# A prompt attention stage with its output projection in two 512-column halves instead of four 256-column quarters

## The chip, the cores and the metric

The kernel runs on one core of a Trainium2 chip. The metric is the device time of one execution in microseconds; three executions of the kernel before gave 1206.93, 1207.19 and 1207.43. The rows below come from one further execution that the hardware profiler recorded.

## The reference, cut to what matters

One decoder layer for a prompt of 1,024 tokens and for 64 sample tokens (8 sequences of 8), with 1,024 channels. A combined input projection feeds a pooling mixer (512 channels) and a sparse attention (8 heads of 64); both outputs are joined, projected and added to the input:

```python
u, q, k, v, qi, ki, wi = project(rms_norm(hp, norm_mix_g[l]), w_in[l])
pool_o = pool_mix(u_ext, 0, pool_w[l], pool_scale[l])
attn_o = dsa_prompt(q, k, v, qi, ki, wi)
hp = hp + jnp.concatenate([pool_o, attn_o], axis=-1) @ w_out[l]
hp = hp + hier_moe(rms_norm(hp, norm_ffn_g[l]), *moe_args)
```

The sample tokens go the same way. The output projection of the prompt, the product with `w_out` in the fourth line, is what the change touches: 1,024 tokens x 1,024 inputs x 1,024 outputs, in float32.

## The kernel before

The stages follow each other: input projections and indexer scores, the index of the sample tokens, **the prompt's attention with its output projection**, the attention of the sample tokens, the experts, the final norm. The change lies in the third, which the profile shows from about 387 to 679 us.

**Work in that stage.** The prompt is cut into tiles of 128 tokens, i = 0 to 7; NT = 8 stands for the 64 sample tokens. Each tile has four pairs of heads, h = 0 to 3, called heads below, and for each pair the two key groups g = 0 and 1. A list `tasks`, written out by a loop, is the order in which PE works; the other engines follow it too, except that they take the turn T(h,1) ahead of the scores S (`tasks_elsewhere`). The tasks are:

- S(i,h): scores of one head pair against 128 (i+1) keys (line 1264) into PSUM banks 0 to 3. DVE adds the mask and takes the maximum (L2369, L2372), ACT takes the exponential (L1799). S is issued one head ahead: S(i,h+1) lies between T(i,h,0) and T(i,h,1).
- T(i,h,g): PE transposes the probabilities in chunks of up to four blocks into banks 4 and 5 in turn (L1275), and ACT copies each chunk out (L1552). From tile 4 on a T has two chunks.
- V(i,h): the probabilities times the values, into bank 6 (L1287). It waits until ACT has copied all chunks of T(i,h,0) and T(i,h,1). Behind V(i,3) DVE inverts the row sums and ACT copies bank 6 out.
- OT(i): PE turns the inverse sums into bank 7 (L1301), and DVE multiplies the attention outputs by them (L2300) into `mixA`, the projection's operand.
- OP(i,q): the output projection of tile i (L1317), eight products of 128 x 128 with a slice of `w_out`, each two records in the trace, into bank 7; DVE adds the result to the residual (L2310). For the sample tokens, OP(8,0 to 3) takes the pooled half alone (four products of 64 rows); OP(8,4) and OP(8,5) take the other half with 512 columns in the next stage (L1311 and L2306).
- SQ(i): ACT squares the sum and takes the root (L1779, L1781), with a load of a table before the root and another before the next exponential. NM(i): DVE normalises (L2315, L2319). XR(i,0), XR(i,1): PE transposes the normalised tile into bank 7 (L1322) and ACT copies it. LG(i): router logits (L1328) into bank 7, which DVE adds up (L2164).

All tasks that use bank 7 (OT, OP, XR, LG) hand it over: the next one starts when the last one's result has been taken out. Every engine works in order. DVE has another job in between: the selection of the sample tokens' keys, cut into pieces (L2017 is the long one), four of them behind every S of tiles 1 to 6; `PIECES` fixes them by S and V and not by OP. GpSimd's L954 and L956 wait for the last of them.

**Where OP stood.** Behind T(i,h,1) and ahead of V(i,h): the quarter 0 of tile i-1 in head 1, 1 in head 2, 2 in head 3, and quarter 3 of tile i-2 in head 0. OT(i-1) and SQ(i-2) follow V(i,0), NM(i-2) follows V(i,1), XR(i-2,0) V(i,2), XR(i-2,1) stands behind T(i,3,0), LG(i-2) behind V(i,3). Behind the last tile a closing list is written out by hand. SP stores the sum h(i) when `last_op(i)` has been added and the normalised tile behind NM(i), and then loads the residual of tile i+2.

Of the kernel before, what the change touches and what calls it, by code (L numbers as in the profile page):

```python
# [18 lines left out]
ALU = mybir.AluOpType  # L19
# [7 lines left out]
NT = SEQ // P  # L27
# [99 lines left out]
def program(nc, x_prompt, x_sample, cache_k, cache_v, cache_idx_k, state_pool, page_table, norm_mix_g, w_in,  # L127
# [5 lines left out]
    with ctx:  # L133
# [6 lines left out]
        ps = ctx.enter_context(nc.psum_tensor("ps", [P, 8, 512], F32))  # L140
# [83 lines left out]
        wout = cut(8 * D, (8, D))  # L224
# [15 lines left out]
        hb = cut(2 * D, (2, D))  # L240
# [28 lines left out]
        hbS = mixP[0:SR, :, 0:256]  # L269
# [150 lines left out]
        for n in range(TILES + 1):  # L420
# [4 lines left out]
            if n:  # L425
                order += [("T1", ("qi", n - 1)), ("T0", ("k", n - 1))]
                i = ORDER[n - 1]
# [39 lines left out]
            return "PT0" if t == ("OP", NT, 5) else "M"  # L467

        def last_op(i):
            return ("OP", i, 3) if i < NT else ("OP", NT, 5)  # L470

        tasks = step("S", 0)
        for i in range(NT):
            for h in range(PAIRS):
                out, old = i - 1, i - 2
                turned, summed, later = [], [], []
                if out >= 0:
                    summed += {0: [], 1: [("OP", out, 0)], 2: [("OP", out, 1)], 3: [("OP", out, 2)]}[h]
                    later += {0: [("OT", out)]}.get(h, [])
                if old >= 0:  # L480
                    turned += {3: [("XR", old, 1)]}.get(h, [])
                    summed += {0: [("OP", old, 3)]}.get(h, [])
                    later = {0: [("SQ", old)], 1: [("NM", old)], 2: [("XR", old, 0)], 3: [("LG", old)]}[h] + later
                tasks += [("T", i, h, 0)] + turned + step("S", i * PAIRS + h + 1) + [("T", i, h, 1)]
                tasks += summed + [("V", i, h)] + later
        i = NT - 1
        tasks += [("OP", i - 1, 3), ("SQ", i - 1), ("OT", i), ("OP", i, 0), ("NM", i - 1), ("OP", i, 1), ("XR", i - 1, 0),
                  ("OP", i, 2), ("XR", i - 1, 1), ("OP", i, 3), ("LG", i - 1), ("SQ", i), ("OP", NT, 0), ("NM", i), ("OP", NT, 1),
                  ("XR", i, 0), ("OP", NT, 2), ("XR", i, 1), ("OP", NT, 3), ("LG", i)]
        tasks_elsewhere = list(tasks)  # L490
        for n, t in enumerate(tasks):
            if t[0] == "S" and n:
# [53 lines left out]
        filled, emptied, use = {}, {}, {}  # L546
# [24 lines left out]
        def take(eng, tag, q, key):  # L571

            eng.wait_ge(filled[tag + q], use[tag, q, key] + 1)
# [464 lines left out]
        def _(pe):  # L1038
            mm = nc.tensor.matmul
# [141 lines left out]
            for n in range(TILES + 1):  # L1181
                if n == 3:
                    pe.wait_ge(state_in, 16)
                    claim(pe, "1", "T0", "state")
                    for g in range(4):
                        ins = tr(ps[:, 0, g * SB * HALO:(g + 1) * SB * HALO], stt_in[0:SB * HALO, g * P:(g + 1) * P], ident(SB * HALO))
# [104 lines left out]
            def tail(t):  # L1291
                kind, i = t[0], t[1]
                r = rows(i)
# [8 lines left out]
                elif kind == "OP":  # L1302
# [11 lines left out]
                    last = 3 if i == NT else 7  # L1314
                    for k in range(last + 1):
                        lhs = mixP[:, k, tok] if k < 4 else mixA[:, k - 4, :]
                        ins = mm(ps[0:r, 7, 0:256], lhs, wout[:, k, 256 * t[2]:256 * t[2] + 256], start=(k == 0), stop=(k == last))  # L1317
                elif kind == "XR":
                    pe.wait_ge(x2_ready, i + 1)
                    for j in range(4):  # L1320
# [621 lines left out]
        def _(dve):  # L1942
            v = nc.vector
# [348 lines left out]
            def tail(t):  # L2292
                kind, i = t[0], t[1]
                r, s = rows(i), i % 2
                if kind == "OT":
                    take(dve, "2b", "M", t)
                    dve.wait_ge(o_kept, i + 1)
                    if i:
                        take(dve, "2b", "M", ("OP", i - 1, 3))
                    v.tensor_tensor(mixA[:, :, :].rearrange("p b q -> p (b q)"), ps[:, 7, :], Osb, ALU.mult).then_inc(emptied["2bM"], 1)  # L2300
                elif kind == "OP":
                    take(dve, "2b", part_of(t), t)
# [3 lines left out]
                        v.tensor_tensor(part, new, part, ALU.add).then_inc(emptied["2b" + part_of(t)], 1)  # L2306
                        return
                    dve.wait_ge(xr_in[s], 16 * (i // 2 + 1))
                    part = hbS[:, t[2], :] if i == NT else hb[0:r, s, 256 * t[2]:256 * t[2] + 256]
                    v.tensor_tensor(part, ps[0:r, 7, 0:256], part, ALU.add).then_inc(emptied["2bM"], 1)  # L2310
                elif kind == "NM":
                    dve.wait_ge(std2_ready, i + 1)
                    if i == 0:
# [233 lines left out]
```

## Time and profile before

| | |
|---|---|
| median of three executions | 1207.19 us |
| the profiled execution, its own time | 1207.76 us |
| its span in the profile | 1205.9 us |
| PE busy in the span | 1084.2 us (90%), 6212 matmul records |
| DVE, ACT, POOL busy | 562.5, 415.3, 233.1 us |
| projection of the prompt and the sample's first half (L1317) | 544 records, 125.6 us |
| mean granted PE clock | 0.954 |

PE is TensorE, PEld its weight loads, DVE VectorE, ACT ScalarE, POOL GpSimd, SP SyncE, and SPq the queue on which SP issues transfers. A row of a timeline gives the start in us from the span's start, the time from the first to the last of its instructions in us, engine, line, operation, what is written and read, how many, and in brackets how long the engine sat idle before it and what released it. A matmul's end is modelled, and a row of several lasts a little longer than the time until the next task starts on PE; so the text takes the pace of PE from starts.

### The profile page before, as it was taken

How to read it: one execution, taken by the hardware profiler on the slowest of the kernel's cores; microseconds unless marked ns; L12 is line 12 of the kernel's file. 1: busy time of each engine (PE TensorE's matmuls, PEld its weight loads, DVE VectorE, ACT ScalarE, POOL GpSimd, SP SyncE). 2: the span in 40 equal slices, each digit the busy share in tenths (PEclk: the TensorE clock that was granted, in tenths of full speed). 3: DMA queues.
4: the chain of work that ended last, by engine and by line, in shares of the span. 5: the costliest groups of instructions: out<-in, count | busy, mean ns of one | idle time of the engine just before them, and what ended most of it. 6: DMA issues, size and time to landing. Idle time of an engine off the chain costs nothing. (4 is left out here: it accounts for less than half of the span.)

```text
span 1205.9 us, 16395 instructions
## 1 busy us (share of the span) xinstructions
PE 1084.2 (90%) x6212; PEld 733.0 (61%) x6212; DVE 562.5 (47%) x1273; ACT 415.3 (34%) x976; POOL 233.1 (19%) x270
## 2 busy tenths in 40 slices
PE   4999989899877899999998799679999999999980
PEld 2554433354444577777776465467778788787860
DVE  3234568999997877666562263111311111111114
ACT  1234445567534355555551143311011111111114
POOL 1433224354422000000004110011212112121210
PEclk9999999999989699999999889879999999999995
DMA  6510000010084111110111472379999999999928
GB/s 219 200 46 12 6 28 1 1 35 5 1 231 154 44 54 53 54 44 28 37 53 61 190 304 84 123 273 348 326 334 343 335 337 346 332 345 333 296 32 304
DMA packets 51198, 191.42 MB, mean 159 GB/s; under 512 B 10910, under 2 KB 13806, under 8 KB 40885
## 3 DMA queue, kind: packets, MB, share of 16 engines
q1 hardware_dynamic: 39439, 142.71, 33.2%
q0 software_dynamic: 11536, 47.71, 14.0%
q8 instruction: 38, 0.62, 0.2%
q14 instruction: 27, 0.22, 0.1%
q10 hardware_dynamic: 158, 0.16, 0.1%
HBM read 162.49 MB, written 28.19 MB: 158 GB/s over the span
## 5 line engine op out<-in xcount | busy, mean ns | idle before, releaser
L1476 PEld LDWEIGHTS ps<-mem 128*128 128x128 f32 x2048 | 236.3, 194 | 16.8 <-issue 16.8
L1552 ACT ACTIVATE mem<-ps 128x512 f32<-128x512 f32 (+9 forms) x344 | 153.2, 487 | 265.2 <-PE ps L1275 61.0
L1476 PE MATMUL ps<-mem 128*128 128x96 f32 x2048 | 235.8, 276 | 0.8 <-DVE mem L2436 0.8
L2017 DVE TENSOR_SCALAR_CACHE_REDUCE mem<-mem 128x768 bf16<-128x768 f32 (+2 forms) x134 | 166.5, 1283 | 0.0
L1317 PE MATMUL ps<-mem 128*128 128x256 f32 (+1 forms) x544 | 125.6, 383 | 6.0 <-ACT mem L1552 2.8
L1482 PE MATMUL ps<-mem 128*96 128x512 f32 x256 | 117.6, 602 | 2.5 <-DVE mem L2428 2.5
L1317 PEld LDWEIGHTS ps<-mem 128*128 128x128 f32 (+1 forms) x544 | 98.7, 187 | 23.4 <-ACT mem L1552 3.7
L2428 DVE TENSOR_TENSOR mem<-mem,ps 128x192 f32<-128x192 f32 x32 | 11.3, 355 | 212.6 <-ACT mem L1892 212.6
L984 POOL DMA_INDIRECT h_rows<-mem x32 | 46.5, 1454 | 295.9 <-DVE mem L2443 295.9
L1892 ACT ACTIVATE mem<-ps 128x192 f32<-128x192 f32 x32 | 10.6, 331 | 262.3 <-PE ps L1476 262.3
L1482 PEld LDWEIGHTS ps<-mem 128*96 128x96 f32 x256 | 39.0, 162 | 57.1 <-issue 51.2
L1106 PE MATMUL ps<-mem 128*128 128x512 f32 (+1 forms) x144 | 70.9, 610 | 0.0
L2369 DVE CUSTOM_DVE_ANT_0 mem<-ps,mem 128x128 f32<-128x128 f32 (+7 forms) x64 | 48.2, 753 | 46.9 <-PE ps L1264 46.8
L2443 DVE TENSOR_SCALAR mem<-ps,mem 96x512 f32<-96x512 f32 x32 | 23.9, 747 | 98.7 <-PE ps L1482 98.7
L1122 PE MATMUL ps<-mem 128*128 128x512 f32 (+1 forms) x192 | 68.1, 505 | 0.0
L1133 PE MATMUL ps<-mem 128*128 128x512 f32 (+1 forms) x144 | 63.5, 593 | 0.0
L1981 DVE SCALAR_TENSOR_TENSOR mem<-mem 128x512 f32<-128x512 f32 (+3 forms) x70 | 46.8, 668 | 19.3 <-ACT mem L1611 14.8
L1275 PE MATMUL ps<-mem 128*128 128x128 f32 x288 | 46.6, 289 | 7.2 <-ACT mem L1799 5.6
L1552 ACT ACTIVATE mem<-ps,mem 96x512 f32<-96x512 f32 (+3 forms) x48 | 29.6, 623 | 67.0 <-PE ps L1482 61.6
L954 POOL TENSOR_TENSOR mem<-mem 64x2056 bf16<-64x2056 bf16 x1 | 4.1, 4071 | 246.6 <-DVEq L2112 246.6
L1611 ACT ACTIVATE mem<-ps 128x512 f32<-128x512 f32 (+3 forms) x80 | 38.4, 522 | 38.2 <-PE ps L1094 34.2
L1122 PEld LDWEIGHTS ps<-mem 128*128 128x128 f32 x192 | 31.3, 194 | 33.1 <-issue 33.1
(299 smaller groups left out, 1448.1 us busy)
## 6 DMA issues: line engine op xcount, KB each, us to landing
mem<-in_expert_w_gate SPq DMA_DIRECT2D x32, 1024.0 KB, 5.1
mem<-in_expert_w_up SPq DMA_DIRECT2D x32, 1024.0 KB, 8.8
mem<-in_expert_w_down SPq DMA_DIRECT2D x32, 1024.0 KB, 13.3
mem<-in_x_prompt SPq DMA_DIRECT2D x16, 512.0 KB, 4.1
mem<-in_w_in SPq DMA_DIRECT2D x3, 2048.0 KB, 10.7
h_rows<-mem SPq DMA_DIRECT2D x8, 512.0 KB, 2.6
xn_rows<-mem SPq DMA_DIRECT2D x8, 512.0 KB, 2.9
mem<-h_rows SPq DMA_DIRECT2D x8, 512.0 KB, 5.4
```

Source lines behind the costliest of these rows:

```text
L984: pool.indirect_dma_start(h_dram, bass.IndirectOffsetOnAxis(ap=slot_dst[0:CAP, e:e + 1], axis=0), out_rows, None, compute_op=ALU.add).then ...
L1106: ins = mm(ps[0:r, 4, :], xnT[:, k, tok], w1[:, k, NKI:NIN - CK], start=(k == 0), stop=(k == KC - 1))
L1122: ins = mm(out, w2[:, k, g * P:(g + 1) * P], xnT[:, k, tok], start=(k == 0), stop=(k == KC - 1))
L1133: ins = mm(ps[0:r, 4, :], xnT[:, k, tok], w2[:, k, CQ:CK], start=(k == 0), stop=(k == KC - 1))
L1275: ins = tr(ps[:, 4 + part, (j - c) * P:(j - c + 1) * P], Sm[:, u % 2, g, j * P:(j + 1) * P], ident(P))
L1317: ins = mm(ps[0:r, 7, 0:256], lhs, wout[:, k, 256 * t[2]:256 * t[2] + 256], start=(k == 0), stop=(k == last))
L1476: ins = mm(ps[:, 2 + s, j * CAP:(j + 1) * CAP], wgu[w][:, j // 2, k, (j % 2) * P:(j % 2 + 1) * P], xgT[:, s, k, :], start=(k == 0), stop=( ...
L1482: ins = mm(ps[0:CAP, 5 + c, :], hT[:, s, k, :], wdn[w][:, k, 512 * c:512 * (c + 1)], start=(k == 0), stop=(k == 1))
L1552: return fn(out, in_, ACT.Copy, scale=scale)
L1981: v.scalar_tensor_tensor(out=dst, in0=src, scalar=wt, in1=dst, op0=ALU.mult, op1=ALU.add).then_inc(score_added, 1)
L2017: v.tensor_scalar(bufs[a % 3][0:R, 0:w], sc, mid[:, a:a + 1], None, ALU.is_ge, ALU.add, accum_out=cnt[:, a:a + 1]).then_inc(step, 1)
L2369: v.tensor_tensor_reduce(out=Sm[:, u % 2, g, 0:w], in0=sc2, in1=maskv(i), scale=1.0, scalar=-3e38, op0=ALU.add, op1=ALU.max, accum_out=mx[ ...
```

## The change

A tile's projection is done in two tasks of 512 columns, each eight products, in place of four of 256. OP(i-1,0) stands in head 1 and OP(i-1,1) in head 3 of tile i; heads 0 and 2 have none. SQ, OT, NM, XR and LG keep their places in the heads. The closing list has two OP of tile 7 and two of the sample tokens, and its order is a new one: XR(6,0) directly behind NM(6), and XR(7,0) and XR(7,1) behind each other. DVE's addition takes 512 columns, and for the sample tokens two quarters of `hbS` at once.

```diff
         def last_op(i):
-            return ("OP", i, 3) if i < NT else ("OP", NT, 5)
+            return ("OP", i, 1) if i < NT else ("OP", NT, 5)
...
                 if out >= 0:
-                    summed += {0: [], 1: [("OP", out, 0)], 2: [("OP", out, 1)], 3: [("OP", out, 2)]}[h]
+                    summed += {1: [("OP", out, 0)], 3: [("OP", out, 1)]}.get(h, [])
                     later += {0: [("OT", out)]}.get(h, [])
                 if old >= 0:
                     turned += {3: [("XR", old, 1)]}.get(h, [])
-                    summed += {0: [("OP", old, 3)]}.get(h, [])
...
-        tasks += [("OP", i - 1, 3), ("SQ", i - 1), ("OT", i), ("OP", i, 0), ("NM", i - 1), ("OP", i, 1), ("XR", i - 1, 0),
-                  ("OP", i, 2), ("XR", i - 1, 1), ("OP", i, 3), ("LG", i - 1), ("SQ", i), ("OP", NT, 0), ("NM", i), ("OP", NT, 1),
-                  ("XR", i, 0), ("OP", NT, 2), ("XR", i, 1), ("OP", NT, 3), ("LG", i)]
+        tasks += [("SQ", i - 1), ("OT", i), ("OP", i, 0), ("NM", i - 1), ("XR", i - 1, 0), ("OP", i, 1), ("XR", i - 1, 1),
+                  ("OP", NT, 0), ("LG", i - 1), ("SQ", i), ("OP", NT, 1), ("NM", i), ("XR", i, 0), ("XR", i, 1), ("LG", i)]
...
-                        ins = mm(ps[0:r, 7, 0:256], lhs, wout[:, k, 256 * t[2]:256 * t[2] + 256], start=(k == 0), stop=(k == last))
+                        ins = mm(ps[0:r, 7, :], lhs, wout[:, k, 512 * t[2]:512 * t[2] + 512], start=(k == 0), stop=(k == last))
...
-                        take(dve, "2b", "M", ("OP", i - 1, 3))
+                        take(dve, "2b", "M", ("OP", i - 1, 1))
...
-                    part = hbS[:, t[2], :] if i == NT else hb[0:r, s, 256 * t[2]:256 * t[2] + 256]
-                    v.tensor_tensor(part, ps[0:r, 7, 0:256], part, ALU.add).then_inc(emptied["2bM"], 1)
+                    new = ps[0:r, 7, :]
+                    if i == NT:
+                        part, new = hbS[:, 2 * t[2]:2 * t[2] + 2, :], new.rearrange("p (q n) -> p q n", q=2)
+                    else:
+                        part = hb[0:r, s, 512 * t[2]:512 * t[2] + 512]
+                    v.tensor_tensor(part, new, part, ALU.add).then_inc(emptied["2bM"], 1)
```

## Rows read from the trace of the kernel before

**Rows 1.** Busy time of PE, PEld, DVE, ACT, POOL; granted clock, DMA share, GB/s.
```profile
412.00:640.00 228.00, 223.67 (x1605) 172.72 (x1606) 150.97 (x366) 118.89 (x239) 4.89 (x2) 1.00 0.12 43
```

**Rows 2.** PE's waits from 385 to 690 us: total us, times, longest.
```profile
PE ps L1287 <- ACT mem L1552: 2.4, 5, 0.6
```

**Rows 3.** Timeline of tile 3, head 0 and what follows it.
```profile
456.98 1.13 PE L1264 MATMUL ps<-mem 64*128 64x512 f32 x4
...
458.04 0.66 PE L1275 MATMUL ps<-mem 128*128 128x128 f32 x4
...
458.53 3.62 PE L1317 MATMUL ps<-mem 128*128 128x256 f32 x16
458.73 0.60 ACT L1552 ACTIVATE mem<-ps 128x512 f32<-128x512 f32 x1 [1.05 <-PE ps L1275]
...
460.39 2.34 DVE L2017 TENSOR_SCALAR_CACHE_REDUCE mem<-mem 64x2056 bf16<-64x2056 f32 x1
...
462.08 1.10 PE L1287 MATMUL ps<-mem 128*64 128x128 f32 x16
...
463.12 0.66 PE L1301 MATMUL ps<-mem 128*128 128x128 f32 x4
...
463.82 0.69 DVE L2300 TENSOR_TENSOR mem<-ps,mem 128x512 f32<-128x512 f32 x1 [0.75 <-PE ps L1301]
...
465.70 3.62 PE L1317 MATMUL ps<-mem 128*128 128x256 f32 x16
```

**Rows 4.** Timeline of tile 0, where V follows the turn directly.
```profile
394.10 0.48 PE L1275 MATMUL ps<-mem 128*128 128x128 f32 x1
394.62 0.28 ACT L1552 ACTIVATE mem<-ps 128x128 f32<-128x128 f32 x1 [0.86 <-PE ps L1275]
...
395.04 0.70 PE L1287 MATMUL ps<-mem 128*64 128x128 f32 x4 [0.46 <-ACT mem L1552]
```

**Rows 5.** Timeline of tile 5: turn of head 0, SQ, turn of head 1.
```profile
524.04 0.87 PE L1275 MATMUL ps<-mem 128*128 128x128 f32 x6
...
524.73 0.87 ACT L1552 ACTIVATE mem<-ps 128x512 f32<-128x512 f32 x2 [1.43 <-PE ps L1275]
...
529.71 1.06 ACT L1779 ACTIVATE mem<-mem 128x1024 f32<-128x1024 f32 x1 [2.28 <-DVE mem L2310]
...
533.10 0.85 PE L1275 MATMUL ps<-mem 128*128 128x128 f32 x6 [0.52 <-ACT mem L1552]
```

**Rows 6.** Timeline of tile 3, head 3: V and the router logits.
```profile
484.27 1.10 PE L1287 MATMUL ps<-mem 128*64 128x128 f32 x16
...
485.58 1.98 PE L1328 MATMUL ps<-mem 128*128 128x36 f32 x16 [0.20 <-DVE mem L2310]
```

**Rows 7.** Timeline of the sample's OP(8,4) and OP(8,5), 512 columns.
```profile
765.48 7.05 PE L1311 MATMUL ps<-mem 128*64 128x512 f32 x16 [0.59 <-ACT mem L1552]
...
769.14 0.68 DVE L2306 TENSOR_TENSOR mem<-ps,mem 64x512 f32<-64x512 f32 x1 [12.13 <-PE ps L1311]
```

**Rows 8.** Timeline of the closing stretch, from LG(5) to LG(7).
```profile
633.37 1.98 PE L1328 MATMUL ps<-mem 128*128 128x36 f32 x16
...
639.18 9.31 POOL L956 TENSOR_SCALAR mem<-mem 64x2048 bf16<-64x2048 bf16 x1
...
645.61 3.72 PE L1317 MATMUL ps<-mem 128*128 128x256 f32 x16 [0.52 <-DVE mem L2310]
645.66 3.25 DVE L2319 SCALAR_TENSOR_TENSOR mem<-mem 128x1024 f32<-128x1024 f32 x1
...
649.85 0.66 PE L1322 MATMUL ps<-mem 128*128 128x128 f32 x4 [0.52 <-DVE mem L2310]
...
666.82 1.28 DVE L2319 SCALAR_TENSOR_TENSOR mem<-mem 128x1024 f32<-128x1024 f32 x1
...
677.12 1.98 PE L1328 MATMUL ps<-mem 128*128 128x36 f32 x16 [0.51 <-DVE mem L2310]
```

**Rows 9.** Busy times and granted clock within the closing stretch.
```profile
664.00:668.00 4.00, 3.49 (x11) 1.64 (x10) 1.67 (x3) 0.00 (x0) 0.00 (x0) 0.57 0.02 7
```

## The prediction, made blind

> **What bounds the kernel now.** I first asked for the busy time by stretch, to find the stage that the edit touches and its bound. Between 412 and 640 us, where tiles 1 to 7 of the prompt attention run, PE is busy 223.7 of 228 us at full clock, DVE 151, ACT 119 [rows 1]. So in this stage a microsecond added to PE's in-order stream, work or wait, lengthens the kernel. The stages behind begin when it has ended and hold no slack that could absorb a shift, so I count it in full. Next I read PE's waits: V behind a turn is the one wait of a kind that the edit multiplies, 5 times for 2.4 us in all, in tiles 0 and 1 [rows 2]. Last I read the order of work in time, tile by tile, on PE, ACT and DVE together.
>
> A head of tile 3 shows the pattern [rows 3]. S starts at 456.98 and takes 1.06 us; T(0,1) starts at 458.04 and takes 0.49; OP(1,3) starts at 458.53 and hands over to V at 462.08, 3.55 us later. Under it ACT copies the turned probabilities, 458.73 to 459.33, and DVE finishes its selection pieces (462.73). V needs that copy and never waits, since OP lies between. That is the cover the edit takes away in every second head. Where no OP stands there already, tile 0, PE waits for it: turn at 394.10, copy done 394.90, V at 395.04 [rows 4].
>
> **Part 1, V behind the turn without OP.** Heads 2 of tiles 1 to 7 and heads 0 of tiles 2 to 7, 13 places, lose their quarter. In tile 3 the copy ends 1.29 us after T starts (0.69 until it starts, 0.60 long) [rows 3], PE is through the turn after 0.49, and V starts some 0.06 after the copy: wait 0.86. With two chunks, as in tile 5, both copies end 1.56 after T starts (524.04 to 525.60) [rows 5] and the turn takes 0.71: wait 0.91. Read so, tiles 1 to 7 give 0.65, 0.75, 0.86, 0.92, 0.91, 0.92, 0.92, in all 5.9 for heads 2 and 5.3 for heads 0: **+11.2**. The lag behind the copy could be 0.14, as in tile 0 [rows 4] (half clock there): 1 us more. Below, if ACT's start lag shrank with nothing else in its queue, 0.2 less each: 2.6 us less. I keep what full clock shows.
>
> **Part 2, OP(i-1,0) behind the scaling of the attention outputs.** Its first matmul needs DVE's multiply behind OT. DVE does that after the masks and pieces of head 0, which OP(i-2,3) used to cover. Tile 3, from the start of S: pieces end at 462.73, +5.75; multiply 0.69 and handover 0.1: OP may start at +6.54. PE gets there at 1.06 + 0.49 + 0.86 (part 1) + 1.04 (V, 462.08 to 463.12) + 2.58 (OT to the next OP, 463.12 to 465.70) = 6.03 [rows 3]: wait 0.5. The same sum is 1.1 for tile 2, and nothing from tile 4 on, where PE's share of the head is longer: **+1.6**. Queued behind on PE is all of head 1, so it is paid once and in full. What is late next on DVE, the masks of head 2, has 7 us of OP as cover. On SP, the store of tile i behind its last OP moves forward by a head's work, and the next residual's load stays behind NM(i), far ahead of its add: nothing waits for either.
>
> **Part 3, the norm on ACT.** SQ (square, table load, root) is no longer released by an OP in head 0; it now follows the two exponentials directly, while PE comes to T(1,1) earlier by the missing OP. With two chunks per turn (tiles 4 to 7) that turn needs the bank that ACT copies only after SQ. Tile 5, from the start of T(0,1): copies end +1.56, two exponentials of 0.94, SQ at +3.56, and T(1,1) can start 3.39 after SQ (529.71 to 533.10) [rows 5], +6.95; PE is there at 5.83 (T 0.71, wait 0.91, V 1.47, OT 0.50, T 0.74, S 1.50). Wait 1.11, against 0.52 to 0.59 in the row [rows 5]. The differences for tiles 4 to 7 are 0.43, 0.52, 0.55, 0.43: **+1.9**. Bounds: 0, if the exponentials end earlier, and 4.
>
> **Part 4, handovers of bank 7.** LG behind V waited in tiles 2 to 5 for a DVE add that stood behind the pieces: in tile 3 V starts 484.27, LG 485.58 [rows 6], 1.31 apart where V takes 1.04 [rows 3]. With 7 us of OP ahead the pieces are done and the add (0.68 instead of 0.41) [rows 7] hides under V: 0.27 saved, 0.33, 0.21 and 0.15 in the others, and 0.13 at OT and XR: **-1.1**.
>
> **Part 5, the matmuls.** 256 columns x 16 records cost 3.55 us [rows 3]. For 512 columns the nearest row is the sample's OP: 16 records in 7.05 us, from 765.48 to 772.53; the add that follows the first eight starts at 769.14, some 0.04 after them, so the second eight take 3.43, 0.429 each [rows 7]. 16 of them to the next task, with the 0.09 that a short block has beyond its records, make 6.95. Columns cost the same either way; a merge saves 0.15. The heads now hold 14 long blocks (97.3) where 27 short ones stood (95.9), as OP(6,3) moves in from the closing stretch: **+1.4**. Weight loads, half as many, stay hidden under the stream.
>
> **Part 6, the closing stretch**, LG(5) to LG(7), 633.37 to 677.12, 43.75 us [rows 8]. Here no V covers anything: an OP costs 4.24 to its successor (645.61 to 649.85) and an XR 1.35 (0.69 + 0.60 + 0.06). In the new order, from LG(5): OT at 2.3, OP(7,0) at 3.8, its add at 10.9. Then NM(6): its normalising instruction took 3.25 instead of 1.28 us, beside a GpSimd instruction that ended at 648.49, and ended 0.4 after that one [rows 8]; starting at 11.7 it still ends that way, at 15.8, for GpSimd's work hangs on DVE's last selection and moves by only 0.3. XR(6,0) now stands directly behind it: PE idles from 11 to 15.9, where OP(7,1) was the cover. Then OP(7,1) at 17.2, XR(6,1) 25.1, OP(8,0) 26.4, LG(6) 30.8, OP(8,1) 33.1, its add 36.7, NM(7) done 38.8, XR(7,0), XR(7,1), and LG(7) at 41.6: **-2.1**, fewer handovers against two uncovered norms. Were the norm not slowed, -4.7.
>
> In a sentence of its own: the Trainium skill ("SBUF — State Buffer", on contention) says that GpSimd and such a VectorE instruction take a shared port for a whole instruction, the loser waiting fully; by that the norm would end 1.28 after GpSimd's and the sum be 0.9 larger, but the row ended 0.4 after it, and I go by the row.
>
> **Part 7, the clock.** It fell to half within 664 to 668 us (granted 0.57 over these 4 us [rows 9], so 1.7 us lost if PE streams there), after short tasks with pauses. A pause of nearly 5 us before OP(7,1) should bring one such stretch more, at the head of 7 us of streaming: **+1.7**; bounds 0 and 3.4.
>
> **Sum**: 11.2 + 1.6 + 1.9 - 1.1 + 1.4 - 2.1 + 1.7 = **+14.6 us**. The span goes from 1205.9 to 1220.5, the profiled time from 1207.8 to 1222.4, the median from 1207.2 to **1221.8**.
>
> **Rivals.** (a) The clock falls again and again: the even heads now carry pauses of 0.9 us among short turns. Each low stretch costs 1.7 [rows 9]; one per even head, 13 of them, gives 22 more, 1244; three more, 1227. Against it: in 412 to 640 it granted 1.00 with pauses present, and long OPs follow every even head. The Trainium skill ("TensorE: Matmul & The Clock Gate", second HAM failure mode) says that small idles between groups of matmuls can make the clock swing; the rows so far do not bear it out for this stage. Chance 0.08.
> (b) Faster: a 512-column record costs less than two of 256. Every 10 ns per pair would be 2.6 us over the 256 pairs of the prompt; from 57 ns on it outweighs all the waits. At 60 ns the time is 1206.4, no change; at 70 ns 1203.9. Against it the pitch of 0.429 [rows 7]; for it only that this row has 64-column weights. Chance 0.03 for faster, 0.03 for equal.
> (c) The copy waits are half hidden, because PE's records hold pauses (their ends are modelled) and the exponentials or copies start earlier: part 1 shrinks to 5.6, time 1216. Tile 0 shows the wait openly, against it. Chance 0.12.
> (d) DVE cannot keep up in even heads: the exponential of the next head is late at T(h+1,0). In tile 3 it is ready some 0.2 us before PE comes. If the masks are 0.5 us late in each of 13, 4 more: 1226. Chance 0.1.
> The forecast itself: 0.64.
>
> **Range.** The bounds of parts 1, 3, 6 and 7 reach from -9 to +5; not all fall together. With (c), (d) and three clock stretches inside: 1214 to 1228. Two measurements of this kernel differ by well under 0.2%, 2.4 us, which I take as what can be told. Faster by more 0.03, within 0.04, slower 0.93.
>
> **What the profile would show.** V records with an idle of some 0.5 to 0.8 us before them, released by ACT's copy, 18 times instead of 5; OP at about 6.95 us from first matmul to V; OP(1,0) and OP(2,0) waiting on DVE's multiply; T(1,1) waiting on ACT 0.7 to 1.4 us in tiles 4 to 6; a gap of over 4 us before XR(6,0), and half clock behind it; no stretch of half clock between 412 and 650. If V follows the turn at once, part 1 and the forecast fall.

## The result and the profile after

The changed kernel takes 1227.33 us, the median of four executions (1225.52 to 1228.73); the kernel before took 1207.06 on the same chip (four, 1205.47 to 1207.43). The ratio is 1.017, interval 1.0152 to 1.0187: slower by 1.7%. The forecast of 1221.8 was low by 5.5 us, inside its range. The profiled execution of after took 1228.73 us with a span of 1226.9, 21.0 more than before.

PE's waits from 385 to 710 us, in the columns of [rows 2]:

```profile
PE ps L1285 <- ACT mem L1550: 12.6, 18, 0.8
PE ps L1320 <- DVE mem L2321: 7.3, 2, 5.0
...
PE ps L1315 <- DVE mem L2298: 2.7, 4, 0.9
PE ps L1273 <- ACT mem L1550: 2.1, 3, 1.0
```

V (L1285) now waits 18 times for ACT's copy where it waited 5 times [rows 2]. XR (L1320) waits 7.3 us for the norm in two places, both in the closing stretch. Windows of after, the first two those of [rows 1] and [rows 9] (the clock is the third number from the end of a line):

```profile
412.00:640.00 228.00, 213.01 (x1318) 125.94 (x1318) 143.81 (x349) 117.09 (x236) 0.00 (x0) 1.00 0.12 42
664.00:668.00 4.00, 2.61 (x6) 1.55 (x7) 0.56 (x1) 0.60 (x1) 0.55 (x2) 0.54 0.60 197
685.00:688.00 3.00, 3.00 (x4) 0.69 (x3) 0.00 (x0) 0.00 (x0) 0.00 (x0) 0.50 0.00 0
695.00:699.00 4.00, 3.60 (x16) 3.48 (x16) 0.20 (x1) 0.00 (x0) 0.00 (x0) 0.50 0.00 0
```

PE is busy 213.0 us of the first window where it was busy 223.7 [rows 1], still at full clock: the window holds 10.7 us more of idle time and not one stretch of half clock. An even head of tile 3, the pattern of [rows 3] without its OP:

```profile
464.41 0.66 PE L1273 MATMUL ps<-mem 128*128 128x128 f32 x4
...
465.10 0.60 ACT L1550 ACTIVATE mem<-ps 128x512 f32<-128x512 f32 x1 [1.05 <-PE ps L1273]
...
465.84 1.10 PE L1285 MATMUL ps<-mem 128*64 128x128 f32 x16 [0.78 <-ACT mem L1550]
...
469.02 0.68 DVE L2298 TENSOR_TENSOR mem<-ps,mem 128x512 f32<-128x512 f32 x1
...
469.85 7.11 PE L1315 MATMUL ps<-mem 128*128 128x512 f32 x16 [0.23 <-DVE mem L2298]
...
476.88 1.10 PE L1285 MATMUL ps<-mem 128*64 128x128 f32 x16
```

The turn starts at 464.41 and V at 465.84. With an OP in between, PE left the turn after 0.49 [rows 3], so the missing cover costs 1.43 - 0.49 = 0.94. The long OP takes 7.03 from start to V (6.96 where it does not wait, as from 485.75 on). The closing stretch, which answers to [rows 8]:

```profile
648.77 1.98 PE L1326 MATMUL ps<-mem 128*128 128x36 f32 x16
...
652.57 7.11 PE L1315 MATMUL ps<-mem 128*128 128x512 f32 x16 [0.88 <-DVE mem L2298]
654.85 9.29 POOL L954 TENSOR_SCALAR mem<-mem 64x2048 bf16<-64x2048 bf16 x1
...
660.51 4.05 DVE L2321 SCALAR_TENSOR_TENSOR mem<-mem 128x1024 f32<-128x1024 f32 x1
664.70 1.08 PE L1320 MATMUL ps<-mem 128*128 128x128 f32 x4 [5.03 <-DVE mem L2321]
666.48 9.44 PE L1315 MATMUL ps<-mem 128*128 128x512 f32 x16 [0.69 <-ACT mem L1550]
...
682.47 1.98 PE L1326 MATMUL ps<-mem 128*128 128x36 f32 x16 [0.78 <-DVE mem L2312]
...
684.73 5.34 PE L1315 MATMUL ps<-mem 128*64 128x512 f32 x8 [0.29 <-DVE mem L2162]
...
692.33 0.63 PE L1320 MATMUL ps<-mem 128*128 128x128 f32 x4 [2.26 <-DVE mem L2321]
...
695.09 3.60 PE L1326 MATMUL ps<-mem 128*128 128x36 f32 x16 [0.78 <-ACT mem L1550]
699.54 0.87 PE L1370 MATMUL ps<-mem 128*128 128x128 f32 x3 [0.85 <-PEq L1356]
```

Read the second column against the first of its kind. OP(7,1) at 666.48 takes 9.44 for the records that OP(7,0) did in 7.11. OP(8,1) at 684.73 takes 5.34; the same eight records take 3.65 at full clock (in the experiment e2 below, which prints them). LG(7) at 695.09 takes 3.60 where LG(6) took 1.98. These are three stretches in which PE streamed at its lower clock (granted 0.54, 0.50 and 0.50 in the windows above), each right behind pauses. The kernel before had one such stretch too, between LG(6) and XR(7,0), where its sample OPs took 2.98 and 2.26 for what later ones did in 1.94, together 1.4 us more. PE's timeline of before:

```profile
663.28 2.98 PE L1317 MATMUL ps<-mem 128*64 128x256 f32 x8 [0.29 <-DVE mem L2164]
666.76 2.26 PE L1317 MATMUL ps<-mem 128*64 128x256 f32 x8 [0.51 <-DVE mem L2310]
...
670.88 1.94 PE L1317 MATMUL ps<-mem 128*64 128x256 f32 x8 [0.69 <-ACT mem L1552]
```

The stages, from starts of PE in both traces (us):

| stretch | before | after | difference |
|---|---|---|---|
| start of the span to the first S | 387.08 | 387.40 | +0.32 |
| heads: first S to LG(5) | 246.29 | 261.37 | +15.08 |
| closing: LG(5) to LG(7) | 43.75 | 46.32 | +2.57 |
| LG(7) to the first matmul of the next stage | 2.68 | 4.45 | +1.77 |
| the rest, to the end of the span | 526.13 | 527.36 | +1.23 |

The sum is 20.97. In the forecast the heads had +15.0; nearly all of what was missing is behind LG(5).

LG(5) is the mark that the forecast used, but the kernel before has OP(6,3) still ahead of it there. The start of OT(7) is the mark by which both kernels have done the same work: from the first S to OT(7) before took 252.79 and after 263.63, +10.8; from there to the next stage 39.93 and 48.51, +8.6. So what the change costs behind OT(7) is nearly as much as what it costs in the heads.

### The profile page after: what moved, and what is told of

It reads as the page before. It is cut to its first block and busy times, and to the rows that moved or that the text cites. A ratio compares the mean times of both kernels' runs of the same rounds, so it can differ in the third digit from the quotient of the medians.

```text
span 1226.9 us, 15815 instructions
## 1 busy us (share of the span) xinstructions
PE 1088.7 (89%) x5940; PEld 686.7 (56%) x5940; DVE 561.6 (46%) x1255; ACT 414.6 (34%) x976; POOL 233.1 (19%) x270
## 5 line engine op out<-in xcount | busy, mean ns | idle before, releaser
L1474 PEld LDWEIGHTS ps<-mem 128*128 128x128 f32 x2048 | 235.5, 193 | 16.7 <-issue 16.7
L1315 PE MATMUL ps<-mem 128*128 128x512 f32 (+1 forms) x272 | 124.3, 610 | 4.4 <-DVE mem L2298 2.7
L1315 PEld LDWEIGHTS ps<-mem 128*128 128x128 f32 (+1 forms) x272 | 50.4, 191 | 66.0 <-issue 60.0
L1104 PE MATMUL ps<-mem 128*128 128x512 f32 (+1 forms) x144 | 70.9, 610 | 0.0
L1120 PE MATMUL ps<-mem 128*128 128x512 f32 (+1 forms) x192 | 68.1, 505 | 0.0
L1131 PE MATMUL ps<-mem 128*128 128x512 f32 (+1 forms) x144 | 63.5, 593 | 0.0
L952 POOL TENSOR_TENSOR mem<-mem 64x2056 bf16<-64x2056 bf16 x1 | 4.1, 4069 | 261.9 <-DVEq L2110 261.9
L1797 ACT ACTIVATE mem<-mem 128x128 f32<-128x128 f32 (+7 forms) x64 | 49.3, 772 | 6.5 <-DVE mem L2374 6.3
L1285 PE MATMUL ps<-mem 128*64 128x128 f32 x576 | 40.3, 283 | 12.6 <-ACT mem L1550 12.6
## 6 DMA issues: line engine op xcount, KB each, us to landing
mem<-in_w_in SPq DMA_DIRECT2D x3, 2048.0 KB, 10.7
```

The costliest lines, as they stand in the source:

```text
L1104: ins = mm(ps[0:r, 4, :], xnT[:, k, tok], w1[:, k, NKI:NIN - CK], start=(k == 0), stop=(k == KC - 1))
L1120: ins = mm(out, w2[:, k, g * P:(g + 1) * P], xnT[:, k, tok], start=(k == 0), stop=(k == KC - 1))
L1131: ins = mm(ps[0:r, 4, :], xnT[:, k, tok], w2[:, k, CQ:CK], start=(k == 0), stop=(k == KC - 1))
L1315: ins = mm(ps[0:r, 7, :], lhs, wout[:, k, 512 * t[2]:512 * t[2] + 512], start=(k == 0), stop=(k == last))
L1474: ins = mm(ps[:, 2 + s, j * CAP:(j + 1) * CAP], wgu[w][:, j // 2, k, (j % 2) * P:(j % 2 + 1) * P], xgT[:, s, k, :], start=(k == 0), stop=( ...
L1797: fn(probs, probs, ACT.Exp, bias=nb[:, c:c + 1], scale=SCALE, accum_out=esum[:, 8 * (i % 2) + c:8 * (i % 2) + c + 1]).then_inc(s_exp, 1)
```

## The experiments

Eleven kernels, all timed. The stretches of each, from its profiled execution; the heads are given from LG(0) to LG(5), because the half clock over tile 0, which lasts longer in some executions than in others, lies ahead of LG(0). In e6 LG(5) stands ahead of V(7,3), so its first two columns would not compare. Ratios are to the kernel before on the same chip.

| kernel | median | ratio (95%) | LG(0) to LG(5) | LG(5) to LG(7) | LG(7) to next |
|---|---|---|---|---|---|
| before | 1207.1 | 1 | 178.76 | 43.75 | 2.68 |
| after | 1227.33 | 1.0170 (1.0152 to 1.0187) | 187.80 | 46.32 | 4.45 |
| e1 heads only | 1227.0 | 1.0169 (1.0136 to 1.0202) | 187.79 | 46.10 | 2.70 |
| e2 closing only | 1208.76 | 1.0023 (1.0007 to 1.0040) | 178.76 | 44.15 | 4.30 |
| e3 both norms ahead | 1216.61 | 1.0078 (1.0048 to 1.0108) | 187.79 | 37.79 | 3.14 |
| e4 other cover | 1224.31 | 1.0133 (1.0100 to 1.0165) | 184.95 | 45.09 | 4.30 |
| e5 root under OP | 1229.5 | 1.0181 (1.0156 to 1.0205) | 189.54 | 46.51 | 4.10 |
| e8 e3, e4 and e5 | 1217.85 | 1.0084 (1.0058 to 1.0110) | 188.15 | 37.88 | 2.65 |
| e7 quarters, new closing | 1206.35 | 0.9991 (0.9982 to 1.0001) | 178.77 | 40.43 | 4.57 |
| e6 halves over two heads | 1207.42 | 1.0001 (0.9989 to 1.0014) | | | 4.29 |
| e9 first norm ahead | 1219.61 | 1.0104 (1.0087 to 1.0121) | 187.77 | 39.16 | 4.30 |
| e10 second norm ahead | 1225.84 | 1.0156 (1.0139 to 1.0173) | 187.81 | 44.85 | 3.03 |
| e11 e4 and e3 | 1214.98 | 1.0067 (1.0043 to 1.0091) | 185.02 | 39.58 | 2.92 |

**e1, the heads of the change with the closing list of before.** Tile 7 and the sample tokens keep quarters, in the old order.

```diff
+        def wide(i):
+            return 256 if i in (NT - 1, NT) else 512
-        tasks += [("SQ", i - 1), ("OT", i), ("OP", i, 0), ("NM", i - 1), ("XR", i - 1, 0), ("OP", i, 1), ...
+        tasks += [("SQ", i - 1), ("OT", i), ("OP", i, 0), ("NM", i - 1), ("OP", i, 1), ("XR", i - 1, 0), ...
```

> Two halves per tile in the heads (OP(0) to OP(6) as in the changed kernel), but tile 7 and the sample tokens in quarters and the closing list in the order of the kernel before. Theory (uncovered turns in the even heads cost 15 us up to LG(5), the new closing list costs the rest, the two add): LG(5) starts some 15 us later than before and the closing stretch is one quarter shorter (4.2 us) than the 43.75 us of before, so the whole is +11 us on the kernel before, about 1218, and some 9 us faster than the changed kernel. Rival (one cause for all, the width of the matmuls or the state of the clock from the heads on): the time stays within 3 us of the changed kernel, 1224 to 1230.

Measured 1227.0, as slow as the change and in the rival's range, not the theory's. The heads kept their +9.0 from LG(0) on, but the old order of the closing stretch no longer was what it had been. Its timeline around the first norm:

```profile
653.04 9.29 POOL L958 TENSOR_SCALAR mem<-mem 64x2048 bf16<-64x2048 bf16 x1
...
655.02 7.73 DVE L2326 SCALAR_TENSOR_TENSOR mem<-mem 128x1024 f32<-128x1024 f32 x1
...
662.67 0.41 DVE L2317 TENSOR_TENSOR mem<-ps,mem 128x256 f32<-128x256 f32 x1
...
663.14 1.12 PE L1324 MATMUL ps<-mem 128*128 128x128 f32 x4 [4.45 <-DVE mem L2317]
```

NM(6) came 2 us behind the start of GpSimd's long instruction and took 7.73 us instead of 1.28; the add of OP(7,1) stood queued behind it on DVE until 662.67, and XR(6,0) behind the add. Before, the norm started 6.5 us after the start of GpSimd's instruction [rows 8] and there was little left to wait for. One OP fewer at the head of the list, OP(6,3), was enough to move it; from OT(7) to the next stage e1 took 46.54 us where before took 39.93. The rival's cause, the width or a clock that is low from the heads on, is not what the trace shows: from 412 to 640 us the granted clock was 1.00, and the loss stands at the norm. So my account of the closing stretch was incomplete: it depends on the phase between DVE's norm and GpSimd's instruction, in the old order too.

**e2, the heads of before with the closing list of the change.**

```diff
+        def wide(i):
+            return 256 if i in (*range(NT - 1),) else 512
-        tasks += [("OP", i - 1, 3), ("SQ", i - 1), ("OT", i), ("OP", i, 0), ("NM", i - 1), ("OP", i, 1), ...
+        tasks += [("OP", i - 1, 3), ("SQ", i - 1), ("OT", i), ("OP", i, 0), ("NM", i - 1), ("XR", i - 1, 0), ...
```

> The converse: the heads in quarters as before (with OP(6,3) as first task of the closing list), tile 7 and the sample tokens in halves with the closing list of the change. Theory: LG(5) starts as before (633.4 us in the span, within 0.5), the closing stretch has the pause of about 4 to 5 us ahead of XR(6,0) and half clock behind it; whole time +7 to +9 us on the kernel before, about 1215. V has no waits behind turns in tiles 2 to 7. Rival (the change costs only through the heads): 1207 to 1208, or 1205 if fewer handovers pay as in my sum without the clock.

Measured 1208.76, +0.23% or 3 us: less than expected. The phase was a kind one, as the timeline of e2's closing stretch shows:

```profile
642.94 9.30 POOL L958 TENSOR_SCALAR mem<-mem 64x2048 bf16<-64x2048 bf16 x1
...
653.11 1.28 DVE L2326 SCALAR_TENSOR_TENSOR mem<-mem 128x1024 f32<-128x1024 f32 x1
...
654.54 0.63 PE L1324 MATMUL ps<-mem 128*128 128x128 f32 x4 [2.26 <-DVE mem L2326]
...
671.80 3.65 PE L1319 MATMUL ps<-mem 128*64 128x512 f32 x8 [0.29 <-DVE mem L2166]
...
681.29 3.60 PE L1330 MATMUL ps<-mem 128*128 128x36 f32 x16 [0.78 <-ACT mem L1554]
```

GpSimd had ended at 652.24, 0.9 ahead of the norm, which took its 1.28, and the pause ahead of XR(6,0) was 2.26 and not 5.03. No half clock followed it: OP(7,1) took 7.13 there. It came at the end, over XR(7,0), XR(7,1) and LG(7). LG(5) started at 637.14 where 633.4 was expected; all of that arose ahead of LG(0), in an execution that was 4 us slower than the median (1212.75): its first S came 1.5 us later and its half clock over tile 0 lasted longer. So the two parts do not add: 20 us for the heads alone, 3 for the closing list alone, 20 for both.

**e3, the change with both norms ahead of an OP.**

```diff
-        tasks += [..., ("OP", i, 0), ("NM", i - 1), ("XR", i - 1, 0), ..., ("OP", NT, 1), ("NM", i), ...
+        tasks += [..., ("NM", i - 1), ("OP", i, 0), ("XR", i - 1, 0), ..., ("NM", i), ("OP", NT, 1), ...
```

> The changed kernel with NM(6) ahead of OP(7,0) and NM(7) ahead of OP(8,1) in the closing list, nothing else. Theory (XR(6,0) idles because the norm stands behind the addition of OP(7,0), and the pause lowers the clock): no pause over 1 us before XR(6,0), no half clock over OP(7,1), NM(7) done under OP(8,1): 4.2 + 2.6 + 1.3 to 3 us less, 1218 to 1219. Rival (VectorE's norm cannot run at all while GpSimd's 9.3 us instruction runs, wherever it stands): the addition of OP(7,0) is then held back too, XR(6,0) starts no earlier than some 16 us after LG(5), and only NM(7) gives 1 to 3 us: 1224 to 1226.

Measured 1216.61, 10.7 less than the change on another chip, and a little under the 1218 to 1219 expected. Within the traces the closing stretch went from 46.32 to 37.79, the step behind it from 4.45 to 3.14: 9.8 less. The timeline of e3 around the first norm:

```profile
652.17 3.31 DVE L2321 SCALAR_TENSOR_TENSOR mem<-mem 128x1024 f32<-128x1024 f32 x1
...
654.48 10.17 POOL L954 TENSOR_SCALAR mem<-mem 64x2048 bf16<-64x2048 bf16 x1
...
660.10 0.66 PE L1320 MATMUL ps<-mem 128*128 128x128 f32 x4 [0.79 <-DVE mem L2312]
```

The norm runs while PE streams OP(7,0), and XR(6,0) waits 0.79, for the add alone. It still took 3.31 us and not 1.28, since it now starts within an earlier instruction of GpSimd (L952, 650.33 to 654.39), but that is under the OP. And now GpSimd's long instruction is lengthened, 10.17 instead of 9.29.

**e9 and e10, each of the two moves of e3 alone.**

> The change with only NM(6) moved ahead of OP(7,0); NM(7) stays behind the sample's second OP. It splits the 10.7 us that both norms moved ahead gave back. Theory: each of the two pauses ahead of an XR pays for itself and for the half clock behind it. Then the stretch LG(5) to LG(6) falls from 33.70 to about 26.7 (5.0 of pause, 2 of half clock behind it), while LG(6) to LG(7) stays near 12.6 and LG(7) to the next stage near 4.4: 7.0 us, 1220 us. Rival: the later half clock, at OP(8,1) and at LG(7), is a consequence of the first pause; then LG(6) to the next stage falls too, from 17.07 to about 14.2, and the time is near 1217.

> The change with only NM(7) moved ahead of the sample's second OP; NM(6) stays behind OP(7,0). Theory: the pause of 5.03 us ahead of XR(6,0) stays, with half clock over OP(7,1), so LG(5) to LG(6) stays 33.7; the pause of 2.26 ahead of XR(7,0) goes, and perhaps half clock behind it: LG(6) to the next stage falls from 17.07 by 1.5 to 3, 1224 to 1226 us. Rival: NM(7) runs into another instruction of GpSimd there, and nothing is gained: 1227.

Both came out by the theory. e9: LG(5) to LG(6) fell from 33.70 to 26.71, by 4.2 of pause (5.03 to 0.78) and 2.8 of half clock; LG(6) to LG(7) stayed (12.62 and 12.45). e10: 33.69 stayed, LG(6) to LG(7) fell to 11.16, and LG(7) to the next stage from 4.45 to 3.03. PE's timeline in the closing stretch of e9, then of e10:

```profile
660.60 7.13 PE L1315 MATMUL ps<-mem 128*128 128x512 f32 x16 [0.69 <-ACT mem L1550]
...
676.55 5.18 PE L1315 MATMUL ps<-mem 128*64 128x512 f32 x8 [0.29 <-DVE mem L2162]
...
686.74 3.60 PE L1326 MATMUL ps<-mem 128*128 128x36 f32 x16 [0.78 <-ACT mem L1550]
```

```profile
667.15 9.43 PE L1315 MATMUL ps<-mem 128*128 128x512 f32 x16 [0.69 <-ACT mem L1550]
...
685.40 5.34 PE L1315 MATMUL ps<-mem 128*64 128x512 f32 x8 [0.29 <-DVE mem L2162]
...
694.30 2.33 PE L1326 MATMUL ps<-mem 128*128 128x36 f32 x16 [0.78 <-ACT mem L1550]
```

The half clock over OP(7,1) goes with the pause of 5.03 (9.43 against 7.13). That over LG(7) shrinks with the pause of 2.26. That over OP(8,1) goes with neither: it is there in after, e3, e9 and e10 (5.34, 5.25, 5.18, 5.34), and in e4, e5, e8 and e11 too, behind OPs and turns that each leave PE 0.7 to 0.8 us idle at the handover of bank 7. Nor is it a cost of the change: in all thirteen traces, before and e1 among them, the clock falls 2 to 8 us behind the start of LG(6), and what differs is which task it falls on.

**e4, other cover for V.** OT in head 0 and XR(i-2,0) in head 2 stand between the turn and V.

```diff
-                    later += {0: [("OT", out)]}.get(h, [])
+                    summed += {0: [("OT", out)]}.get(h, [])
+                    summed += {2: [("XR", old, 0)]}.get(h, [])
```

> The changed kernel with OT(i-1) in heads 0 and XR(i-2,0) in heads 2 moved from behind V to between T(h,1) and V, so that 0.5 us of other PE work lies in each wait for ACT's copy; same work. Theory (V waits 0.65 to 0.9 us for the copy in 13 places, and that wait is worth its full length): in the 13 heads 0 and 2 with such a task the wait before V falls from 0.8 to 0.3 us, in all 5 to 6 us less, about 1221 to 1222. Rival (the recorded pauses before V are in part the modelled ends of matmuls, or PE would wait anyway further on): under 2 us gained, 1225 to 1228.

Measured 1224.31, between the two ranges. PE's waits from 412 to 655 us, in the columns of [rows 2]:

```profile
PE ps L1286 <- ACT mem L1551: 4.9, 13, 0.6
PE ps L1274 <- ACT mem L1551: 4.0, 4, 1.4
PE ps L1316 <- DVE mem L2299: 2.8, 3, 1.3
```

After has 10.2, 2.1 and 2.7 in their place. V waits 5.3 us less with half a microsecond of other work ahead of it; 1.9 of that comes back at the turn behind SQ, to which PE now comes earlier. From LG(0) to LG(5) 2.85 was kept. The closing stretch has the clock on other tasks than in after: a low stretch lies on OP(7,0), which takes 8.80, and the pause ahead of XR(6,0) is 3.33.

**e5, the root under the long OP.** SQ moves from behind V(i,0) to behind the OP of head 1.

```diff
+                    summed += {1: [("SQ", old)]}.get(h, [])
-                    later = {0: [("SQ", old)], 1: [("NM", old)], ...
+                    later = {0: [], 1: [("NM", old)], ...
```

> The changed kernel with SQ(i-2) moved from behind V(i,0) to behind OP(i-1,0), so that ACT does its 2.7 us of square, table load and root under the 7 us of OP, behind the two exponentials. Theory: T(i,1,1) no longer waits for ACT in tiles 4 to 7 (in the changed kernel 1.0, 0.8 and 0.3 us are recorded, and I priced the four at 3.7): LG(5) starts 2 to 4 us earlier, the whole 1223.5 to 1225. Rival (OP(i-1,0) then waits for something else that ends just as late, VectorE's multiply behind the selection pieces): tiles 2 and 3 unchanged, under 1 us gained in tiles 4 to 7.

A miss: 1229.5, and the heads 1.7 us longer. The wait at T(1,1) was gone as expected, but the waits from 412 to 655 us held new ones:

```profile
PE ps L1321 <- ACT mem L1551: 3.2, 6, 0.5
...
PE ps L1274 <- ACT mem L1798: 1.0, 3, 0.5
```

and ACT's timeline in tile 5 shows why:

```profile
545.31 1.28 ACT L1780 ACT_TABLE_LOAD   x1
546.60 0.29 ACT L1780 ACTIVATE mem<-mem 128x1 f32<-128x1 f32 x1
...
553.88 1.28 ACT L1798 ACT_TABLE_LOAD   x1
555.18 0.94 ACT L1798 ACTIVATE mem<-mem 128x768 f32<-128x768 f32 x1
```

A root costs ACT two table loads of 1.28, one to it and one back. In the change the one back was under the long OP of head 1 (542.04). Behind the move the next exponential is that of head 3, and the load stands ahead of it in the short head 2, where nothing long runs on PE. I had hidden the first load and uncovered the second.

**e8, e3 to e5 together.**

> Halves in heads 1 and 3 as in the change, with all three repairs: OT and XR ahead of V, SQ under OP, both norms ahead in the closing list. Theory (the three causes are separate and all lie on PE's path): the repair of the closing list gave 10.7 us; V's waits halve (5.3 us), and now that SQ is out of the way nothing of it comes back at T(i,1,1) (1.9 us were given back there), plus SQ's own 2 us: 7 us under the 1216.6 of the kernel with norms ahead alone, 1209 to 1211; still slower than the kernel before by 2 to 5 us, because half of V's waits and those of OP on VectorE stay. Rival (what the heads lose is the emptier schedule of VectorE, which no reordering mends): 1213 or more.

A miss: 1217.85 where 1209 to 1211 was expected. The closing repair held (37.88), the repairs of the heads cancelled out (188.15 against 187.80). With OT and XR(i-2,0) moved, the table load of e5 is met by a still earlier PE: the turn (L1275) waits for the exponential 4.6 us in six places, up to 1.1. Ahead of LG(0), in tile 2, the clock fell as well (granted 0.57 from 452 to 456 us), behind waits of 1.05 and 0.53 that followed each other within 3 us; no other of these kernels has that.

**e11, e4 with both norms ahead, SQ left where it was.**

> The change with OT and XR(i-2,0) moved between the turn and V in heads 0 and 2 (3 us less alone), and both norms of the closing stretch moved ahead (10.7 less alone); SQ stays behind V. Theory: the two repairs are in different stretches and add up: 1213.5 us, LG(0) to LG(5) 185, LG(5) to LG(7) 37.8. Rival: the square and the root on ACT, which the moved OT now delays in tiles 4 to 7, reach into the closing stretch and cost a microsecond: 1214.5 or more. In neither case is it the time of before.

Measured 1214.98 (1213.94 to 1218.64). The heads took 185.02, as expected; the closing stretch 39.58 instead of 37.8, since a stretch of half clock lay on OP(7,0), a clock of 0.61 granted over 650 to 654 us (OP(7,0) took 8.80, as in e4, which shares the other cover). The rival's number fits, its mechanism is not in the trace: SQ(6) ended ahead of the norm.

**e6, halves split over two heads.** The eight products of a half are issued four in one head and four in the next, so that every head has cover again; LG moves ahead of the turn T(i,3,1), and the closing list is new.

```diff
-                    summed += {1: [("OP", out, 0)], 3: [("OP", out, 1)]}.get(h, [])
+                    summed += {1: [("OA", out, 0)], 2: [("OP", out, 0)], 3: [("OA", out, 1)]}.get(h, [])
+                    summed += {0: [("OP", old, 1)]}.get(h, [])
...
-                    for k in range(last + 1):
+                    for k in range(first, min(last + 1, halfway)):
```

> Halves of 512 columns, each split by its eight products over two heads (four in one head, four in the next, adding up in bank 7), so that every head keeps 3.5 us of OP ahead of V; LG moved to between S and T(i,3,1); closing list as in the kernel with quarters and a new closing list. Theory (the width costs nothing, the missing cover does): no waits of V behind turns in tiles 2 to 7, LG-to-LG intervals as before or up to 0.3 us shorter for fewer handovers: 3 to 6 us faster than the kernel before, about 1202. Rival (512 columns or the accumulation across heads cost something by themselves): the heads are slower than before by over 0.5 us per tile, total 1208 or more.

Measured 1207.42, ratio 1.0001. In the heads no V waits for ACT, and the cover is four 512-column products where it was eight of 256. The timeline of e6 in tile 3, head 0:

```profile
458.39 0.66 PE L1276 MATMUL ps<-mem 128*128 128x128 f32 x4
458.88 3.60 PE L1328 MATMUL ps<-mem 128*128 128x512 f32 x8
462.41 1.10 PE L1290 MATMUL ps<-mem 128*64 128x128 f32 x16
```

3.53 us for the block, where the short one took 3.55 [rows 3]: on PE the width is worth next to nothing. What makes the change slow there is where the block stands, not how wide it is. The gain of 5 us that I expected on top did not come. By the mark of OT(7) the traces show where it stayed out. The closing part is as good as that of e7 below (38.67 from OT(7) to the next stage, e7 38.50, before 39.93), but from the first S to OT(7) e6 took 254.86 where before took 252.79. So 2.1 of the change's 10.8 us are left, or new. PE's waits from 412 us to OT(7) show them, 6.7 us in all against 4.5 in before. 0.9 is a wait of LG(5), which in its new place needs an ACT copy at once:

```profile
629.25 1.95 PE L1341 MATMUL ps<-mem 128*128 128x36 f32 x16 [0.90 <-ACT mem L1565]
```

1.4 more are waits of 0.1 to 0.3 of OT(1) to OT(4) and XR(0,0) to XR(2,0) for the 512-column add, where none waited in before; 0.6 is saved at LG(0) to LG(2). The rival, over 0.5 us per tile and 1208 or more, is not met either.

**e7, the heads of before and a closing list with halves for tile 7 and the sample tokens**, in which each norm stands ahead of an OP.

> Heads in quarters as before; only the closing list is new: tile 7 and the sample tokens in halves, each norm and its transposes with an OP or an XR of the other tile between them. Theory (handovers of bank 7 cost 0.7 to 0.8 us each with nothing to cover them, and VectorE's norm is held up by GpSimd's 9.3 us instruction only where it starts inside it): LG(5) as in the kernel before, from there to LG(7) 40 to 42 us where before takes 43.75, no pause over 1.5 us on PE, clock at full rate up to LG(7): 2 to 4 us faster than the kernel before. Rival (the pauses and low stretches of the clock in the closing list come whatever its order): within 1 us of the 1208.8 of the kernel with the change's closing list.

Measured 1206.35, ratio 0.9991 with an interval that reaches 1.0001: the closing stretch fell by 3.3 us, as expected, but the step behind it took 4.57 instead of 2.68, so 1.4 us were left, about what the ratio shows. (The profiled execution gained only 0.4 in its span: it was 2.1 later at the first S, where the kernels do not differ, and 1.2 faster behind.) LG(7) ran at half clock, though no wait behind LG(5) was longer than 0.88:

```profile
676.08 3.60 PE L1330 MATMUL ps<-mem 128*128 128x36 f32 x16 [0.78 <-ACT mem L1554]
```

This is the best of the kernels that I ran, and not clear of no change.

## Why the prediction was right, and where it was short

**Part 1, V without cover: +11.2, measured +12.3.** Shown. From starts, turn to V less turn to OP, the 13 places cost 0.73, 0.83, 0.83, 0.94, 0.95, 0.99, 1.00 and then 1.0 each. The error is the lag from the end of the copy to V: 0.14 (465.70 to 465.84), the upper bound that I had named, and not 0.06.

**Part 2, OP(i-1,0) behind the multiply: +1.6, measured +1.4**, 0.99 in tile 2 and 0.40 in tile 3.

**Part 3, SQ on ACT: +1.9, measured +0.7.** In tile 5, T(0,1) starts at 533.81, SQ at 537.11 and T(1,1) at 540.49. The 3.38 from SQ to the turn is that of [rows 5]; SQ started 3.30 after the turn and not 3.56, because the two exponentials now stand back to back behind the copy. With V a tenth later too, the extra wait in tiles 4 to 7 was 0.10, 0.16, 0.27 and 0.20. The waits themselves were 1.01, 0.68 and 0.41 in tiles 4 to 6, where I had named 0.7 to 1.4.

**Part 4, bank 7: -1.1, measured -1.0.** LG follows V without a wait from tile 2 on (0.85, 1.03, 1.26, 1.47 after it, against 1.15, 1.31, 1.46, 1.62).

**Part 5, the matmuls: +1.4, measured +1.8.** 14 long blocks took 97.8 us, 27 short ones 96.0. The sample's row [rows 7] held for 128-column weights: 6.96 against 6.95.

So the heads came to +15.1 against +15.0, with errors of +1.1 and -1.2 in two terms that cancelled. That this sum is right is partly luck; each mechanism was seen where it was forecast.

**Part 6, the closing stretch: -2.1.** Its mechanism held: XR(6,0) started 15.93 behind LG(5) (forecast 15.9), after a pause of 5.03, and where the clock was full the steps were those of the forecast but for 0.3 in all (41.9 without the low clock, against 41.6). What I read of the norm was right in its end and thin in its reason. Beside GpSimd it ended 0.42 us behind the end that the trace records for GpSimd's instruction, in before, after and e1 (648.91 and 648.49; 664.56 and 664.14; 662.75 and 662.33), whatever its own start: it does not run slowly beside it, it waits. The Trainium skill ("SBUF — State Buffer", on contention) has this as a lock that the loser waits out in full. These rows bear it out, with one addition: the norm's own 1.28 must begin 0.86 before the recorded end of this instruction of GpSimd, so the 0.9 us that I had charged to that rule was not due.

**Part 7, the clock: +1.7, measured +6.2.** This is the term that was short. The 41.6 of Part 6 held all steps at full clock; LG(5) to LG(7) took 46.32, 4.5 of it for the clock, and LG(7) to the next stage 1.8 more than before. By place: 2.76 over XR(6,0) and OP(7,1), 1.70 over OP(8,1), 1.77 over LG(7). Two things were wrong. First, I allowed for one stretch, at the price of [rows 9], 1.7; the one behind the pause cost 2.8, as it lasted longer (OP(7,1), 10.22 from start to the next task where 7.9 was forecast, shows 2.3 for itself), and there was one more, over LG(7). Second, I called mine "one such stretch more", but set a list without any against 43.75 us that held the 1.4 of before's own stretch. At full clock the two lists differ by 0.5 and not by 2.1; with before's stretch kept in both, the forecast would have been about +16.0. The stretch over OP(8,1) takes the place of that one. The one over LG(7) shrinks where the second pause goes (e10), but it also comes without that pause (e6, e7). My bound of 3.4 was too low.

The sum: 14.6 + 4.5 for the clock + 0.3 in Part 6 + 0.1 in the heads + 0.3 ahead of the first S + 1.2 behind the closing stretch = 21.0. I can't assign the 1.2. After has a stretch of half clock among the experts that before has not (eight of their records took 5.37 at 872.24), but e2, e6, e7 and e11 have it too, and there that part took 524.4 to 525.7 us, less than the 526.1 of before.

**The rivals.** (a) had the size, "three more, 1227", but not the place: from 412 to 640 us the granted clock was 1.00, with 13 pauses. (b) is excluded by Part 5 and by e6. (c) would have shown a smaller Part 1; it was larger. (d): T(h+1,0) never waits for the exponential from tile 1 on; it does in e5 and e8, where the table load stands ahead of it.

**Open.** Why the clock falls behind LG(6) in every kernel, on OP(8,0) in before and e1, on OP(8,1) in eight others and later in e2, e6 and e7; and what else the fall over LG(7) hangs on. I saw what preceded them and did not vary that alone.

## What to carry to other kernels

A matmul that needs an engine's copy of what PE has just made costs the whole copy, its start lag and the lag behind it (here 1.43 us from turn to V), unless other work of at least that length stands between; merging two blocks of work into one wide one saved next to nothing on PE (6.96 against twice 3.55) and takes the cover from every second place. When a block moves, follow what stood in its shadow: a second table load, a norm, a store. Cost a pause at more than its length where PE has no long stream around it: 5 us of pause brought about 2.8 more at half clock, and a repair that removed the pause gave both back. And when a forecast adds low stretches to a list, count those that the old list has already.

## What the runs showed of the hardware that I had not expected

- DVE's norm, 1.28 us alone, took 2.35, 3.25, 4.05 and 7.73 us when it started within GpSimd's instruction of 9.3 us (e4, before, after, e1), and ended 0.40 to 0.43 behind the recorded end of the other each time. Behind the start of GpSimd's earlier one of 4.1 us (e3, e8, e9, e11) it took 3.3 and ended 1.1 behind that one's end, so the 0.42 is not a rule for every pair; GpSimd's next instruction then took 10.17 instead of 9.29.
- The price of one list of tasks hangs on that phase. The old list took 43.75 us in before and 46.10 in e1, though e1 has an OP fewer in it; the new one took 46.32 in after and 44.15 in e2, with an OP more.
- 13 pauses of 0.57 to 0.84 us, one in every second head among long streams, left the granted clock at 1.00. In the closing stretch it fell to 0.54 behind a pause of 5.03 us and, in e11, to 0.61 behind pauses of 0.29 and 0.88; in e7 it was 0.50 over 676 to 680 us with no wait over 0.88 ahead. Before and after the change alike it fell behind LG(6).
